# Hybrid gMLP / RG-LRU encoder on eight cores: the first tile of the last pass moved into the stage before it, with later gate matmuls and a subtile-by-subtile output order

## The reference

```python
for l in range(DEPTH):                                   # DEPTH = 2
    h = _rmsnorm(x, norm1_g[l])
    z = h @ w_in[l]                                      # (B,S,6*1024): u | v | lru_x | lru_gate | gate_A | gate_B
    y_a = gelu(u) * (w_s @ layernorm(gelu(v)) + b_s)     # chunks of 128 positions
    xc = conv(lru_x)                                     # taps at offsets -1, 0, +1, +2
    y_b = (_rglru_scan(xc, ..., False) + _rglru_scan(xc, ..., True)) * gelu(lru_gate)
    x = x + (sigmoid(gate_A) * y_a + sigmoid(gate_B) * y_b) @ w_out[l]
    h = _rmsnorm(x, norm2_g[l])
    gu = h @ w_ffn_in[l]
    x = x + (silu(gu[..., :D_FF]) * gu[..., D_FF:]) @ w_ffn_out[l]
return _rmsnorm(x, final_g)

def _rglru_scan(x32, w_r, b_r, w_i, b_i, lam, reverse):
    r, i = sigmoid(blockdiag(x32, w_r, b_r)), sigmoid(blockdiag(x32, w_i, b_i))   # 8 blocks of 128 x 128
    log_a = -8 * r * softplus(-lam)
    a, mult = exp(log_a), sqrt(1 - exp(2 * log_a))
    # h_t = a_t * h_(t-1) + mult_t * (i_t * x_t), over the whole sequence, from the left or from the right
```

## Time and profile before

| | us |
|---|---|
| median of 3 runs (4122.54 to 4664.74) | 4124.24 |
| the profiled execution | 4136.46 |
| its span, slowest core (core 1) | 4134.9 |
| spans of the eight cores | 4063.2 to 4134.9 |
| PE busy, share of the span | 3747.6, 91% |
| DVE busy | 2467.1, 60% |
| ACT busy | 2210.1, 53% |
| second pass, from about 840 to | 2631 |
| ninth round and tile 0 up to its FFN | 2631 to 2838 |
| the rest of the last pass | 2838 to 4135 |

### The profile page before, as it was taken

One profiled execution on the slowest core, in us unless ns is written; L12 is line 12 of the kernel. 1 busy time (PEld: TensorE's weight loads), 2 busy tenths in 40 slices (PEclk: granted clock), 3 DMA queues, 4 the chain that ended last, 5 costly groups with the idle time before them and its releaser, 6 DMA issues.

```text
span 4134.9 us, 56456 instructions; the slowest of 8 cores (4063.2 to 4134.9 us)
## 1 busy us (share of the span) xinstructions
PE 3747.6 (91%) x17826; PEld 1706.4 (41%) x17826; DVE 2467.1 (60%) x3625; ACT 2210.1 (53%) x3252; POOL 350.3 (8%) x594
## 2 busy tenths in 40 slices
PE   5788888798999998999999999868999999999988
PEld 2333333343444444444444444323444444444443
DVE  4777777754657665665766666465565555645533
ACT  5777787743646547464645746485453443524211
POOL 3111111010100010010001000000000000000000
PEclk9888789899999999999999999988999999999999
DMA  9877778789787979878787776664667576575653
GB/s 197 150 143 135 138 158 179 223 163 244 214 223 235 233 246 220 257 207 231 225 231 246 226 243 196 202 212 145 210 230 236 184 235 208 198 249 158 199 166 102
DMA packets 368257, 836.92 MB, mean 202 GB/s; under 512 B 37264, under 2 KB 153184, under 8 KB 358880
## 3 DMA queue, kind: packets, MB, share of 16 engines
q1 hardware_dynamic: 252224, 767.25, 58.9%
q0 software_dynamic: 115744, 66.07, 14.2%
HBM read 748.27 MB, written 206.58 MB: 231 GB/s over the span
## 4 chain that ended last, share of the span: by engine, by line
PE 73%; DMA 11%; ACT 6%; issue 4%; DVE 4%; POOL 1%; SPq 0%; ACTq 0%; DVEq 0%; POOLq 0%
PE pfall L1186 26%; PE pfall L1004 17%; PE pfall L1208 14%; PE pfall L986 4%; PE pfall L1162 4%; PE pfall L956 3%; DMA HB<-ib 3%; PE pfall L1234 2%; DMA YA<-guth 2%; PE pfall L711 2%; DMA xs<-x 2%; DVE ib L746 1%; PE pfall L622 1%; DMA wzx<-w_in 1%; DMA xr<-XL 1%
## 5 line engine op out<-in xcount | busy, mean ns | idle before, releaser
L1186 PE MATMUL pfall<-hTa,wr 128*128 128x512 bf16 x2816 | 636.3, 385 | 5.4 <-ACT guth L1006 3.8
L1186 PE MATMUL pfall<-hTb,wr 128*128 128x512 bf16 x2816 | 621.0, 381 | 2.7 <-ACT hTb L1176 2.7
L1208 PE MATMUL pfall<-wr,ff 128*128 128x512 bf16 x2816 | 611.7, 379 | 0.0
L1004 PE MATMUL pfall<-hTa,wr 128*128 128x512 bf16 x1920 | 435.3, 382 | 2.0 <-ACT guth L1006 2.0
L1186 PEld LDWEIGHTS pfall<-hTa,wr 128*128 128x128 bf16 x2816 | 278.3, 99 | 345.6 <-issue 30.0
L1186 PEld LDWEIGHTS pfall<-hTb,wr 128*128 128x128 bf16 x2816 | 276.4, 98 | 338.1 <-issue 8.7
L1208 PEld LDWEIGHTS pfall<-wr,ff 128*128 128x128 bf16 x2816 | 275.5, 98 | 332.3
L1213 DVE SCALAR_TENSOR_TENSOR xr<-pfall,xr 128x512 f32<-128x512 f32 x128 | 79.5, 684 | 385.1 <-PE pfall L1208 385.1
L898 DVE SCALAR_TENSOR_TENSOR xm<-zb,cols,xm 128x512 f32<-128x512 f32 x384 | 277.2, 747 | 52.8 <-ACT hz L1241 20.8
L1162 PE MATMUL pfall<-wr,mT 128*128 128x512 bf16 x1024 | 239.8, 394 | 67.1 <-DVE mT L1151 42.7
L1004 PEld LDWEIGHTS pfall<-hTa,wr 128*128 128x128 bf16 x1920 | 187.3, 99 | 223.1 <-issue 12.2
(11 more groups left out here) (167 smaller groups left out, 5178.7 us busy)
## 6 DMA issues: line engine op xcount, KB each, us to landing
wr<-WB SPq DMA_DIRECT2D x832, 512.0 KB, 5.2
XC<-xm SPq DMA_DIRECT2D x32, 1024.0 KB, 8.0
YA<-guth SPq DMA_DIRECT2D x128, 256.0 KB, 5.1
xm<-XC SPq DMA_DIRECT2D x32, 1024.0 KB, 9.1
ya<-YA SPq DMA_DIRECT2D x128, 256.0 KB, 6.3
WB<-w_ffn_in POOLq DMA_DIRECT2D x44, 512.0 KB, 13.6
WB<-w_in POOLq DMA_DIRECT2D x32, 512.0 KB, 31.2
HF<-ib SPq DMA_DIRECT2D x16, 1024.0 KB, 8.1
```

Of the source, the lines that this page charges most:

```text
L1004: op = sc.mm(key, p, [(lambda e, k=k: e.matmul(p.f(), lhsT=w(k), rhs=hT[:, k, lo:lo + TT], start=(k == 0), stop=(k == KC - 1)), bh + [bw]) ...
L1186: op = sc.mm(keyf(t), p, [(lambda e, k=k, o=o, q=q, p=p: e.matmul(p.f(), lhsT=q[:, k, o:o + 128], rhs=hT[:, k, 0:TT], start=(k == 0), stop ...
L1208: sc.mm(keyf(nb, q, s), ps[s], [(lambda e, f=f, s=s, t=t, q=q, p=ps[s]: e.matmul(p.f(), lhsT=fs[f][0][:, s * 128:(s + 1) * 128], rhs=t[:, ...
```

## The change

1. Second pass: `R0` c moves behind `FI` 10 + 3c//2 (10, 11, 13, 14, 16, 17, 19, 20).
2. `FO` in another order (`last=True`), for tile 0 of layer 0 and for all tiles of the last pass: the half nb = 0 as before, the half nb = 1 subtile by subtile. In tile 0 of layer 0 the layer 1 transposes `T1` of subtiles 0 and 1 are put among them (`T1L`).
3. The ninth round gets a list of its own (`lastseq`): all `R1` and `LONE` first, then `V`, then for each c the forward gates `RF` with `U` and `GA`, then `G0` and `B0` for all c, which were in the group G3. The forward recurrence of tile 0 reads an input tile of its own (`XF`, where the x tiles of layer 0 lay) and writes an `ib` of its own (`ibf`, where the last four weight buffers lay, so that the weight ring has 7 buffers in this round). `ra` stays shared. `merge` of tile 0 reads `hT1`, which is still in SBUF, so that its load from HBM goes.
4. Last pass, tile 0: `G` and `B` of tile 1 for c = 0 and 1 stand between the `T2` instead of behind `FI` 10 and 11.

```diff
@@ merge
+        hb, bhb = ib, bib
-        sc.op("dve", lambda e: e.tensor_add(out=hf, in0=hf, in1=ib[:, c, :]), 0.68, reads=[bhf, bib[c]], writes=[bhf])
+        sc.op("dve", lambda e: e.tensor_add(out=hf, in0=hf, in1=hb[:, c, :]), 0.68, reads=[bhf, bhb[c]], writes=[bhf])
@@
-    def fseq(extra):
+    def fseq(extra, last=False):
         r = []
         for f in range(FC):
             r += [("FI", f, 0), ("FI", f, 1)] + [t for a, t in extra if a == f]
+        if last:
+            r += [("FO", 0, q, s) for q in range(6) for s in range(NS)]
+            for s in range(NS):
+                r += [("FO", 1, q, s) for q in range(6)]
+                if s >= 2:
+                    r += [("T1L", s - 2)]
+            return r
         return r + [("FO", nb, q, s) for nb in range(2) for q in range(6) for s in range(NS)]
+
+    def lastseq():
+        r = [("R1", c) for c in range(KC)] + [("LONE", 0)]
+        r += [("V", s, nb) for s in range(NS) for nb in range(2)]
+        for c in range(KC):
+            r += [("RF", c), ("U", c), ("GA", c)]
+            if c >= 2:
+                r += [("GM", c - 2)]
+        r += [("GM", 6), ("GM", 7)]
+        for c in range(KC):
+            r += [("G0", c), ("B0", c)]
+        return r
@@ second pass
-            if xtp is not None and c in T1AT:
+            if xtp is not None and c in T1AT and (j >= 0 or T1AT[c] >= 2):
                 tok += [("T1", T1AT[c])]
-            a, late = aseq()
             if j < 0:
-                a = [t for t in a if t[0] != "R1"]
-                for n, c in enumerate(range(KC)):
-                    a.insert(2 + n + n // 2, ("R1", c))
-                a.insert(20, ("LONE", 0))
+                a = lastseq()
+            else:
+                a, late = aseq()
-                extra += [(int(7 + 1.7 * c), ("R0", c)) for c in range(KC)]
-            tok += fseq(extra)
+                extra += [(10 + 3 * c // 2, ("R0", c)) for c in range(KC)]
+            tok += fseq(extra, j == 0)
-        if j >= 0:
+        if j < 0:
+            wring = TR("wr", 7, [128, 2048], BF16, 0)
+        else:
@@ last pass
-    G3 = G2 + NT + 1
+    G3 = G2 + NT
-    h1load(0)
-    rgates(1, 0, 0, wgf1, lambda c: (G3, 1.0 + 2 * c))
-    recur(1, 0, XM8, ra, bra, ib, bib, car3, True)
-    mT = [mixer(c, 0, (G3, 2.0 * c), (G3, 2.0 * c + 0.5), gu8, th3) for c in range(KC)]
+    XF = XMTile(T("xf", [128, 8, TT], F32, 48 * K, nsub=8), [0, 1])
+    for h in range(2):
+        xcload1(0, XF, h)
+    ibb, bibb = ib, bib
+    ib, bib = T("ibf", [128, KC, TT], F32, 28 * K, nsub=KC)
+    xgates(1, 0, XF, wgf1[0], wgf1[1], lambda c: K0["RF", c])
+    recur(1, 0, XF, ra, bra, ib, bib, car3, True)
+    mT = [mixer(c, 0, K0["G0", c], K0["B0", c], gu8, th3) for c in range(KC)]
+    ib, bib = ibb, bibb
+    wring = TR("wr", WRN, [128, 2048], BF16, 0)
@@ last pass, tile 0
-            tok += [("T2", s) for s in range(NS)]
-            gat = {10 + c: c for c in range(KC)}
+            for s in range(NS):
+                tok += [("T2", s), ("GB"[s % 2], s // 2)]
+            gat = {10 + c: c for c in range(2, KC)}
@@
-        tok += fseq(extra)
+        tok += fseq(extra, True)
         if j == 0:
             for c in range(KC):
                 tok.insert(tok.index(("FO", c // 6, c % 6, NS - 1)) + 1, ("R", c))
```

More of the change, by code:

```diff
@@ L1400, in _build @@
         if xtp is not None:
-            norm1_next(j + 1, xtp, lambda s: K_["T1", s])
+            norm1_next(j + 1, xtp, lambda s: K_["T1", s] if ("T1", s) in K_ else K_1["T1L", s])
             xtp = None
-        if j >= 0:
+        if j < 0:
+            wring = TR("wr", 7, [128, 2048], BF16, 0)
+        else:
             hfr = TR("hf", 3, [128, TT], F32, HVA)
@@ L1431, in _build @@
             apart(ja, K_)
-            if j < 0:
-                first_column(K_["LONE", 0])
         if j < 0:
+            first_column(K_["LONE", 0])
+            K0 = K_
             continue
@@ L1457, in _build @@
             hT1 = split_bufs(*T("h1", [128, KC, TT], BF16, A_HT + HTB), NS)
-        xtp = xt
-    G3 = G2 + NT + 1
+        xtp, K_1 = xt, K_
+    G3 = G2 + NT
     wgf1 = gate_weights(1, 0, A_128)
     car3 = [None]
-    hTa = split_bufs(*T("hTa3", [128, KC, TT], BF16, A_HT), NS)
     def h1load(j):
@@ L1469, in mixer @@
     def mixer(c, j, key0, key1, gur, thr):
-        return merge(1, c, j, (key0, key1), hTa[0], 0, hTa[1], sgx.block(c), sgb.block(c), gur, thr)
+        h, bh = hT1 if j == 0 else hTa
+        return merge(1, c, j, (key0, key1), h, 0, bh, sgx.block(c), sgb.block(c), gur, thr)
     hfr = TR("hf", 3, [128, TT], F32, HVA)
@@ L1476, in _build @@
     mTr = TR("mT", 8, [128, TT], BF16, QX + 18 * K)
-    h1load(0)
     sgx, sgb = Stream(1, "g"), Stream(1, "gB")
-    rgates(1, 0, 0, wgf1, lambda c: (G3, 1.0 + 2 * c))
-    recur(1, 0, XM8, ra, bra, ib, bib, car3, True)
-    mT = [mixer(c, 0, (G3, 2.0 * c), (G3, 2.0 * c + 0.5), gu8, th3) for c in range(KC)]
+    XF = XMTile(T("xf", [128, 8, TT], F32, 48 * K, nsub=8), [0, 1])
[8 more added lines that the diff above has]
+    wring = TR("wr", WRN, [128, 2048], BF16, 0)
+    hTa = split_bufs(*T("hTa3", [128, KC, TT], BF16, A_HT), NS)
     bgr = TR("bg3", 5, [128, TT], F32, QX + 8 * K)
-    xr5 = Ring([T(f"xr3{i}", [128, D], F32, a) for i, a in enumerate([48 * K, 52 * K, 56 * K, 60 * K, QX + 26 * K])])
+    xr5 = Ring([T(f"xr3{i}", [128, D], F32, a) for i, a in enumerate([QX + 26 * K, 48 * K, 52 * K, 56 * K, 60 * K])])
     sgr = Ring([T("sg3a", [128, TT], F32, QX + 30 * K), T("sg3b", [128, TT], F32, 44 * K)])
@@ L1528, in _build @@
             mT = []
-            if not gat:
-                mT = [mixer(c, j + 1, K_["G", c], K_["B", c], bgr, bgr) for c in range(KC)]
+            mT = [mixer(c, j + 1, K_["G", c], K_["B", c], bgr, bgr) for c in range(2 if gat else KC)]
         norm2(xt, lambda s: K_["T2", s], hTb[0], hTb[1], g2, bg2)
```

## The result

The changed kernel takes 4067.9 us (median; the kernel before, run beside it, 4130.6). The ratio is 0.9849, with a 95% interval from 0.9814 to 0.9885: about 63 us less, where 114 were forecast, and 6 us above the upper end of the range. It is faster for certain, and by less than 2%.

A forecast was written before the change was run, and what follows sets the result against it. PE's order was taken to set the end, with gains only from PE waits and the half clock behind them. Terms 52 + 28.3 + 28 + 5.5 = 113.8 off 4136.5 gave 4022.7, median 4010 us; 8-in-10 range 3982 to 4062.

The forecast's parts named there:

- Bound: Whole kernel: PE's order sets the end, so gains come only from PE waits and the half clock behind them.
- Later R0 gates, 52: Second pass, first FI to first FO: gates three blocks later find load and store done or almost; gain 52 us.
- The slowest core: Core 3, 68 us ahead, gains some 25 us less, so core 1 stays the one that counts or draws level.
- The rival of the waits that move with the gates: Second pass: load and store land later, gates' gain falls from 52 to about 10, time 4052 us; chance 0.12.
- The ninth round, 28.3: Stage from layer 0's last FO through tile 0's start of the last pass: three gains, together 28.3 us.
- FO by subtile: Before the ninth round: only subtile 3's chain stays bare between FO's end and Z, 6.8 us; gain 7.9.
- From Z to OP's end: Ninth round: trailing forward work of tile 0 before OP goes, about 3 us remain behind the last tanh; gain 13.5.
- The block of G and B: Tile 0, last pass: four groups of G and B stand in T2's gaps and not in FI; gain 6.9 us.
- The table loads: ACT in the ninth round: 24 loads of 1.28 us; six switches more would cut the stage from 28.3 to 20.6.
- FO by subtile in the last pass, 28: Output projections of tiles 1 to 7 no longer stop for the x tile; gain 28 us, bounds 12 and 33.
- The weights, whose order was the feared price: Subtile-wise FO: weight chunks needed faster; price taken as zero, bound 3 us a tile; slower rival 4142 us, chance 0.04.
- The tail, 5.5: Kernel's end: of four final norms in a row only subtile 3's is left; gain 5.5 us.

The follow-up runs named there:

- the cast edit: The changed kernel with the casts of R0's input blocks not queued on ACT ahead of the FFN block their gate follows: 4040.6 us, ratio 0.9782 to before.

## Why the prediction was wrong

**Bound.** That PE's order sets the end, and that a gain comes from PE's waits, held: each gain in the table but the tail's is a wait of PE or half clock that went.

**Later R0 gates, 52: this is the step that failed.** It followed the waits of the gate on PE and found that neither depends on PE's place in the FFN. That was nearly right: the load slipped by one block and the gate moved by three, so load and gate now meet, and L711 hardly waits. It left out that the cast is an instruction of ACT's queue, with the FFN's tanhs behind it. The cast stood two FI blocks ahead of its gate before and four after, so it waited for the load when PE no longer did, and stopped FI through PSUM. The term gave 28.7, and the runs with the cast moved returned 16 to 19 us of the 23 that were missing. The row was there: ACT idle for 10.67 us in front of the cast, put down only to the gate. The gates' own share was right: back at the old place they cost some 40 us (4064.8 against the 4024.5 of the same chip, which differs besides by R 6 and R 7).

**The slowest core.** The prediction let core 1 draw level with core 3, since the fast cores had less to gain. In fact each pair has one core with late loads, another one from execution to execution, and the time is that of the worst of four. On the other cores the forecast of 79.9 per tile nearly came true (480.6 to 486.9 for the six tiles, most of the excess in the first of them).

**The rival of the waits that move with the gates** named a price of 42 us and a cause, loads that slip. The price was 23. The load did slip, by 3 to 4 us in most tiles and 8 in one, but hardly past the gate's new place: the wait that moved is the cast's, and it fell on the FFN's matmuls.

**The ninth round, 28.3.** FO by subtile gave 5.8 of 7.9, of which 1.2 is a reading: the prediction took FO's end at 2631.4, and the row's length gives 2632.6. From Z to OP's end it was 12.5 of 13.5; OP stops for 8.0 us instead of the 3 left to it, and starts earlier than thought. The block of G and B gave 8.8 in FI but cost 3.2 in T2's gaps, net 5.6 of 6.9: they don't fit into the gaps for nothing. Together 23.9, the 15.0 and 8.8 of the table.

**The table loads.** 22 from FO's end to the first FI, where the kernel before has 25 (the prediction's 24 end at OP; up to there it is now 18). One takes 1.28 us, and the activation behind it starts at its end (the load at 1364.56 and the tanh at 1365.85, above). The Trainium skill ("ScalarE: Activation LUTs", What ACT_TABLE_LOAD costs) adds a drain of 1.38 us to each switch; no row here shows one, and with fewer loads than before the two recurrences among gelus cost nothing in this term.

**FO by subtile in the last pass, 28.** Between the two slowest cores it gave 23.7 less the 4.7 of tile 0; the prediction read its loss on core 1, which had the most to gain of the eight. The wait of 23.7 us on `xr` went as forecast. Two prices were set too low: the evictions of the four subtiles now hold up the first group of G (7.3 us in six waits, L1004 on L1166), and R 6 and R 7 in the last subtile cost 3 to 5 us, of which the prediction left 3 for both. The weights, whose order was the feared price, were never late in an FO.

**The tail, 5.5.** 4.5.

**Not forecast.** 9.3 us up to the first FO. 2.7 of them are in the first tile's FI, where PE waits 2.1 us for a load of `wsn` (0.3 before). The other 6.6 stand before the first FI, where the change does nothing. The first FI is at 845.1 and 828.8 on cores 1 and 3 before, and at 851.7, 833.8 and 834.0 on cores 3, 1 and 4 after. It differs so much from core to core; the cause stays open.

## What to carry to other kernels

A wait for a load belongs to the queue in which the waiting instruction stands, not only to the work it feeds: moving the consumer on one engine gains only a part (here 28.7 us of 52), while the cast, copy or activation that prepares its operand still sits early in the queue of another. When you move work, list each engine's instructions behind the one that waits, and move the preparing instruction with its consumer. And read the gain from the core that will be the slowest afterwards, in the role it then has.

## What the runs showed of the hardware

While POOL's copies run beside the loads, one of two neighbouring cores lands its loads late, and which one changes between executions (cores 0, 3, 4 and 6 in the first trace of the changed kernel, 1, 3, 4 and 6 in the one on chip 3): with the cast edit on chip 1 cores 0, 2, 4 and 6 have spans of 4033 to 4039 us, and the other four 3998 to 4001.

```profile
core 6: 4033.3 us, clock 0.965
core 7: 4000.9 us, clock 0.967
```

The loads of `xm`, 1 MB each, land there after 19.8 us (median) on core 6, and after 12.2 on core 7; with POOL's copies out of its way, on chip 2, they take 7.5 on core 2 and 7.4 on core 3, and neighbours' spans differ by 13 to 21 us only. In the stretch of that load the DMA share of core 3 of the changed kernel is 1.05 (columns as in the stretches above):

```profile
1370.00:1380.00 10.00, 5.88 (x28) 2.45 (x25) 0.00 (x0) 1.21 (x3) 0.00 (x0) 1.00 1.05 281
```

The row shows the stop as a whole: PE 5.88 of 10 us, DVE none, ACT 1.21, all for one load. The clock stayed at 1.00, but the first matmuls behind the stop ran partly at half: 24 take 6.78 us, where 24 at full clock take 5.34; the granted clock is 0.57 from 1380 to 1384 and 1.00 behind that.
